# Hybrid attention trunk on one core: an attention step that takes both heads of a pair and a quarter of the tokens

## The reference, cut to what matters

```python
def nsa_mixer(...):                      # layer 0, 2 groups of 8 heads share keys
    s_c = einsum('bqghd,bngd->bghqn', qb, k_cmp); p_c = masked_softmax(s_c, cmp_end <= t)
    s_s = einsum('bqghd,bgqkd->bghqk', qb, k_s);  p_s = masked_softmax(s_s, m_s)
    s_w = einsum('bqghd,bkgd->bghqk', qb, k_w);   p_w = masked_softmax(s_w, m_w)
    o = gb[..., 0:1] * o_c + gb[..., 1:2] * o_s + gb[..., 2:3] * o_w
def dsa_mixer(...):                      # layer 1, one key and value for all 16 heads
    score = where(pos <= t, einsum('bqh,bqhs->bqs', wib, relu(qib @ ki)), NEG_INF)
    _, sel = lax.top_k(score, 256)
    s = einsum('bqhd,bqkd->bhqk', qb, k[sel]); p = masked_softmax(s, sel <= t)
    o = einsum('bhqk,bqkd->bqhd', p, v[sel])
for i in range(2):
    x = x + rms_norm(mixer(rms_norm(x, g0)), g1)
    x = x + rms_norm(conv_ffn(rms_norm(x, g2)), g3)
```

## Time and profile before

| | before |
|---|---|
| median of 3 runs | 3346.78 us (3346.12 to 3353.05) |
| the profiled execution's own time | 3344.59 us |
| its span in the profile | 3342.8 us |
| instructions in the span | 37464 |
| mean granted TensorE clock | 0.943 |

### The profile page before, as it was taken

One profiled execution on the slowest core, in us unless ns is written; L12 is line 12 of the kernel. 1 busy time (PEld: TensorE's weight loads), 2 busy tenths in 40 slices (PEclk: granted clock), 3 DMA queues, 4 the chain that ended last, 5 costly groups with the idle time before them and its releaser, 6 DMA issues.

```text
span 3342.8 us, 37464 instructions
## 1 busy us (share of the span) xinstructions
PE 2987.1 (89%) x13312; PEld 2293.7 (69%) x13312; DVE 2076.4 (62%) x3708; ACT 1512.6 (45%) x2609; POOL 278.1 (8%) x221
## 2 busy tenths in 40 slices
PE   7797999999879999999987676379997999999997
PEld 5685666666567888878865564255666788887885
DVE  6544445555166766687766699754426777667666
ACT  4342555545444444445433455444434454444443
POOL 2352000000000000000002024130000000000000
PEclk9787999999999999999998788689998999999999
DMA  5143121121332333333323012452132333333332
GB/s 167 44 105 99 43 54 41 43 49 36 101 89 76 95 99 97 95 94 96 95 70 110 7 41 87 107 140 51 33 114 69 90 96 97 96 95 95 103 103 73
DMA packets 362770, 275.17 MB, mean 82 GB/s; under 512 B 64230, under 2 KB 314152, under 8 KB 362072
## 3 DMA queue, kind: packets, MB, share of 16 engines
q1 hardware_dynamic: 361431, 270.68, 28.1%
q10 hardware_dynamic: 1152, 2.10, 0.2%
HBM read 238.18 MB, written 31.92 MB: 81 GB/s over the span
## 4 chain that ended last, share of the span: by engine, by line
PE 76%; DVE 13%; issue 4%; ACT 3%; DMA 2%; SPq 1%; POOL 0%; POOLq 0%; DVEq 0%; ACTq 0%
PE PS L490 18%; PE PS L492 18%; PE PS L491 18%; PE PS L899 10%; PE PS L822 3%; PE PS L877 3%; PE PS L875 3%; DVE m_MASK L2271 2%; PE PS L881 1%; DVE m_Z L2345 1%; DVE RT_b L595 1%; DVE m_PRED L2276 1%; PE PS L644 1%; PE PS L893 0%; DMA WR<-in_dsa_w_out 0%
## 5 line engine op out<-in xcount | busy, mean ns | idle before, releaser
L490 PE MATMUL PS<-HH,WH 128*128 128x512 f32 (+1 forms) x2160 | 857.1, 397 | 88.8 <-POOL WL L463 44.6
L491 PE MATMUL PS<-HL,WH 128*128 128x512 f32 (+1 forms) x2160 | 848.6, 393 | 0.0
L492 PE MATMUL PS<-HH,WL 128*128 128x512 f32 (+1 forms) x2160 | 847.9, 393 | 0.0
L490 PEld LDWEIGHTS PS<-HH,WH 128*128 128x128 f32 x2160 | 414.5, 192 | 183.0 <-issue 51.7
L491 PEld LDWEIGHTS PS<-HL,WH 128*128 128x128 f32 x2160 | 414.3, 192 | 86.8 <-issue 2.5
L492 PEld LDWEIGHTS PS<-HH,WL 128*128 128x128 f32 x2160 | 413.1, 191 | 86.1
L479 DVE TENSOR_TENSOR WL<-WR,WH 128x1024 fp32r<-128x1024 f32 x290 | 354.1, 1221 | 109.7 <-ACT WH L472 97.9
L472 ACT ACTIVATE WH<-WR 128x1024 fp32r<-128x1024 f32 x290 | 308.1, 1062 | 125.1 <-PE PS L492 90.0
L919 ACT ACTIVATE n_PX<-PS 128x512 f32<-128x512 f32 (+3 forms) x400 | 186.7, 468 | 257.5 <-PE PS L881 206.1
L1013 DVE CUSTOM_DVE_ANT_0 n_JUNK<-PS,n_MZ 128x512 bf16<-128x512 f32 (+2 forms) x320 | 148.7, 488 | 133.7 <-PE PS L822 131.8
L899 PE MATMUL PS<-m_PX,m_V 128*128 128x512 f32 (+3 forms) x384 | 164.4, 511 | 10.7 <-ACT m_PX L919 10.7
(11 more groups left out here) (375 smaller groups left out, 5358.2 us busy)
## 6 DMA issues: line engine op xcount, KB each, us to landing
WR<-in_ffn_w_up SPq DMA_DIRECT2D x176, 512.0 KB, 3.8
WR<-in_ffn_w_down SPq DMA_DIRECT2D x88, 512.0 KB, 3.6
WH<-qh_save SPq DMA_DIRECT2D x64, 256.0 KB
n_RB<-r_save SPq DMA_DIRECT2D x96, 128.0 KB, 3.0
WR<-in_nsa_w_out SPq DMA_DIRECT2D x16, 512.0 KB, 4.1
WL<-ql_save SPq DMA_DIRECT2D x32, 256.0 KB
WR<-in_dsa_w_in SPq DMA_DIRECT2D x16, 512.0 KB, 4.1
WR<-in_dsa_w_out SPq DMA_DIRECT2D x16, 512.0 KB, 4.1
```

The source lines that it names most:

```text
L490: nc.tensor.matmul(dst, wh, xh, start=start, stop=False)
L491: nc.tensor.matmul(dst, wh, xl, start=False, stop=False)
L492: return nc.tensor.matmul(dst, wl, xh, start=False, stop=stop)
```

## The change: what it does

A unit is now both heads of the pair, one key block, and the tokens of a quarter (256) that see it: `q` takes the place of `h`. Its scores are two runs (one per head) of `w` = 256 or 128 columns that lie side by side in one bank, so a unit has 512 or 256 columns. Queries are read as two runs 512 columns apart; a mask matmul covers the same token block of both heads (256 columns), with the identity read twice; the outputs of a quarter go to two runs of one bank. A group is a branch and a quarter. Its denominators are copied in another order, and its outputs by two copies of 64x256 in place of one of 64x512. The two DMAs of denominators go to 64 partitions each, 32 bytes to a partition, in place of 128 partitions and 16 bytes. The planner's cost goes without its floor of 0.7, and the tables of layer 1 are restated for the smaller number of steps. "cmp" units, peaks, DVE's work and the DMAs of queries, shifts and spreads are the same.

```diff
@@ -92,20 +92,21 @@
+QUARTER = HALF // 2
-def key_blocks(hf, kind):
-
-    blocks = []
-    for kb in range(4 * hf + 4):
-        low = max(kb, 4 * hf)
-        high = 4 * hf + 3 if kind == "full" else min(kb + 4, 4 * hf + 3)
-        diag = kb >= 4 * hf
-        far = kind == "near" and high == kb + 4
-        blocks.append((kb, (low - 4 * hf) * P, (high - low + 1) * P, diag, far))
-    blocks.sort(key=lambda b: b[2] < HALF)
+def key_blocks(hf, q, kind):
+
+    blocks, i0 = [], 4 * hf + 2 * q
+    for kb in range(i0 + 2):
+        low = max(kb, i0)
+        high = i0 + 1 if kind == "full" else min(kb + 4, i0 + 1)
+        if high >= low:
+            far = kind == "near" and high == kb + 4
+            blocks.append((kb, (low - i0) * P, (high - low + 1) * P, far))
+    blocks.sort(key=lambda b: b[2] < QUARTER)
...
-            cost = 3.4 if u.kind == "cmp" else max(0.7, 1.6 * u.w / HALF + dense * u.w / P)
+            cost = 3.4 if u.kind == "cmp" else 1.6 * u.w / QUARTER + dense * 2 * u.w / P
...
+        def both_heads(W, n):
+            o = n.q * QUARTER + n.c0
+            return W[:, n.r % 3, :].rearrange("p (h t) -> p h t", h=2)[:, :, o:o + n.w]
+
+        def both_parts(tile, n):
+            return tile[:, 0:2 * n.w].rearrange("p (h t) -> p h t", h=2)
...
-                nc.tensor.matmul(dst, KA[:, g, keys], query_high(n.r, n.h, n.c0, n.w),
-                                 start=True, stop=False)
-                last = nc.tensor.matmul(dst, KB[:, g, keys], query_low(n.r, n.h, n.c0, n.w),
+                nc.tensor.matmul(dst, KA[:, g, keys], both_heads(WH, n), start=True, stop=False)
+                last = nc.tensor.matmul(dst, KB[:, g, keys], both_heads(WL, n),
                                         start=False, stop=not masks)
+                ones = B["IDB"][:, :].unsqueeze(1).broadcast_to([P, 2, P])
                 for x, (ii, mask) in enumerate(masks):
                     o = ii * P - n.c0
-                    last = nc.tensor.matmul(PS[:, u % 3, o:o + P], mask, B["IDB"][:, :],
+                    last = nc.tensor.matmul(dst[:, :, o:o + P], mask, ones,
                                             start=False, stop=x == len(masks) - 1)
...
-                last = nc.tensor.matmul(PS[:, 6 + n.g % 2, n.c0:n.c0 + n.w], V[:, g, n.kb, :], probs,
+                dst = PS[:, 6 + n.g % 2, :].rearrange("p (h t) -> p h t", h=2)[:, :, n.c0:n.c0 + n.w]
+                last = nc.tensor.matmul(dst, V[:, g, n.kb, :], both_parts(B["PX"][:, u % 4, :], n),
                                         start=n.first, stop=n.last)
...
-                b, o = 6 + n.g % 2, 64 * n.h
-                nc.scalar.activation(DR[o:o + 1, slot, :], PS[64:65, b, :], ACT.Copy)
-                nc.scalar.activation(OP[o:o + 64, slot, :], PS[0:64, b, :], ACT.Copy).then_inc(a_ov, 1)
+                b, o = 6 + n.g % 2, 64 * n.q
+                nc.scalar.activation(DR[o:o + 1, slot, :].rearrange("o (p h j) -> o h p j", h=2, j=4),
+                                     PS[64:65, b, :].rearrange("o (h p j) -> o h p j", h=2, j=4), ACT.Copy)
+                for h in range(2):
+                    last = nc.scalar.activation(
+                        OP[64 * h:64 * h + 64, slot, n.q * QUARTER:(n.q + 1) * QUARTER],
+                        PS[0:64, b, h * QUARTER:(h + 1) * QUARTER], ACT.Copy)
+                last.then_inc(a_ov, 1)
...
-                    for h in range(2):
-                        sp.dma_start(a.B["R4"][:, slot, h, :],
-                                     a.B["DR"][64 * h:64 * h + 1, slot, :]).then_inc(a_chain[slot], 16)
+                    for x in range(2):
+                        row = a.B["DR"][64 * x:64 * x + 1, slot, :]
+                        if plan.units[s].kind == "cmp":
+                            sp.dma_start(a.B["R4"][:, slot, x, :], row).then_inc(a_chain[slot], 16)
+                        else:
+                            sp.dma_start(a.B["R4"][64 * x:64 * x + 64, slot, :, :],
+                                         row).then_inc(a_chain[slot], 16)
...
-        LATE_MASKS = {3: 4, 14: 5, 25: 6, 36: 7}
+        LATE_MASKS = {2: 4, 10: 5, 19: 6, 27: 7}
-        LATE_LOADS = {6 * m + 1: m for m in range(PAIRS)}
-        LATE_HIGHS = {6 * m + 9: m for m in range(PAIRS)}
-        LATE_SAVES = {6 * m + 12: m for m in range(PAIRS)}
+        LATE_LOADS = {9 * m // 2 + 1: m for m in range(PAIRS)}
+        LATE_HIGHS = {9 * m // 2 + 7: m for m in range(PAIRS)}
+        LATE_SAVES = {9 * m // 2 + 9: m for m in range(PAIRS)}
```

More of the change, by code:

```diff
@@ L94 @@
 ROUNDS = 2 * PAIRS
-Unit = namedtuple("Unit", "r kind h kb c0 w diag far first last g rb")
+QUARTER = HALF // 2
+Unit = namedtuple("Unit", "r kind q kb c0 w far first last g rb")
 Peak = namedtuple("Peak", "r kind h ii c")
-def key_blocks(hf, kind):
-    blocks = []
-    for kb in range(4 * hf + 4):
-        low = max(kb, 4 * hf)
-        high = 4 * hf + 3 if kind == "full" else min(kb + 4, 4 * hf + 3)
-        diag = kb >= 4 * hf
-        far = kind == "near" and high == kb + 4
-        blocks.append((kb, (low - 4 * hf) * P, (high - low + 1) * P, diag, far))
-    blocks.sort(key=lambda b: b[2] < HALF)
+def key_blocks(hf, q, kind):
[7 more added lines that the diff above has]
+    blocks.sort(key=lambda b: b[2] < QUARTER)
     return blocks
@@ L118, in attention_units @@
             if kind == "cmp":
-                units.append(Unit(r, kind, 0, 0, 0, HALF, False, False, True, True, groups, rb))
+                units.append(Unit(r, kind, 0, 0, 0, QUARTER, False, True, True, groups, rb))
                 groups += 2
                 continue
-            for h in range(2):
-                blocks = key_blocks(order[r][1], kind)
-                for x, (kb, c0, w, diag, far) in enumerate(blocks):
-                    units.append(Unit(r, kind, h, kb, c0, w, diag, far, x == 0, x == len(blocks) - 1,
+            for q in range(2):
+                blocks = key_blocks(order[r][1], q, kind)
+                for x, (kb, c0, w, far) in enumerate(blocks):
+                    units.append(Unit(r, kind, q, kb, c0, w, far, x == 0, x == len(blocks) - 1,
                                       groups, rb))
@@ L850, in scores_pe @@
                 pe.wait_ge(a_ex, a.qk0 + u - 2)
-            dst = PS[:, u % 3, 0:n.w]
             if n.kind == "cmp":
+                dst = bank(u % 3)
                 for h in range(2):
@@ L863, in scores_pe @@
             else:
+                dst = both_parts(PS[:, u % 3, :], n)
                 KA, KB = (B[x] for x in a.keys[n.kind][0:2])
@@ L867, in scores_pe @@
                 for ii in range(n.c0 // P, (n.c0 + n.w) // P):
-                    i = 4 * hf + ii
+                    i = 4 * hf + 2 * n.q + ii
                     if "MASK" in B and i >= 2:
@@ L888, in values_pe @@
             pe.wait_ge(a_ex, a.qk0 + u + 1)
-            probs = B["PX"][:, u % 4, 0:n.w]
             if n.kind == "cmp":
+                probs = B["PX"][:, u % 4, :]
                 if n.g:
@@ L918, in exp_act @@
                 act.wait_ge(a_pv, a.qk0 + u - 3)
-            nc.scalar.activation(a.B["PX"][:, u % 4, 0:n.w], PS[:, u % 3, 0:n.w],
+            nc.scalar.activation(a.B["PX"][:, u % 4, 0:2 * n.w], PS[:, u % 3, 0:2 * n.w],
                                  ACT.Exp).then_inc(a_ex, 1)
@@ L933, in evict_act @@
             act.wait_ge(a_pv, a.qk0 + u + 1)
-            if n.h == 0 and n.rb >= a.ns:
+            if n.q == 0 and n.rb >= a.ns:
                 act.wait_ge(a_tm, a.rb0 + n.rb - a.ns + 1)
```

## The result

The changed kernel takes **3311.4 us** (median of four runs, 3309.4 to 3314.2) against 3346.7 for the kernel before beside it: ratio 0.9891, 95% interval 0.9874 to 0.9908. In a later series of runs the same kernel gave 3315.3 against 3346.4, ratio 0.9905 (0.9891 to 0.9918). So it is 31 to 36 us faster, where 20 were forecast. The median lies at the low end of the forecast's range (3311), and by the first ratio the kernel stands at 3310.3, just under it.

A forecast was written before the change was run, and what follows sets the result against it. PE was taken to bound most of attention, with ACT and DVE in its shadow. Terms -18 + 2.7 - 4.3 + 0 = -20 us against the profiled 3344.6 gave 3324.6, median 3327 us; range 3311 to 3343.

The forecast's parts named there:

- seam: Matmuls that read or write two runs: taken as free; rival that it costs 19 ns each gives 3357 us, chance 0.10.
- -18 for steps: Layer 0: fewer steps and mask turns save 2.3 us per pair, 18 us for eight, ends 15 and 23.
- +2.7 for evictions: Layer 0: each group's eviction grows by 170 ns, bare only at 16 places before "cmp"; low end 0.
- I take 0.02 off each: Layer 0: 20 masked steps per pair that stay have shorter turns to f32 weights, 0.4 us a pair.
- a step costs 0.05 us beyond its columns: PE in attention: a step without a mask takes 1.33 us, of which columns make 1.28.
- PE's waits: Layer 0: a pair goes from 70.7 to about 68.7 us, by -2.3 for steps and +0.34 for evictions.
- -4.3 forecast: Layer 1, second half: two steps less and 14 shorter turns, 0.54 us per round, eight rounds; ends 2 and 8.
- Nothing else in it waits: Layer 1, second half: no waits beside the steps that are priced, so only 0.54 us per round falls.
- the ring: Layer 1, first half: it holds three peaks; bunching turns a burst of 8 into 12, up to 2.2 us more.
- over 118 us: Sign to check: if layer 1's first half takes longer than this, the ring is the cause.
- I take 0: Layer 1, first half: 2 us saved by sixteen fewer steps set against the ring; net nothing, between -5 and +6.
- as many issues ... nothing: SP and DMAs: the number of issues stays and no wait in the steady pairs hangs on them, so no time.

The follow-up runs named there:

- inter: The changed kernel with the two heads interleaved column by column in a unit: 3307.2 us, ratio 0.9880.
- m128: The changed kernel with each 256-column mask matmul issued as two of 128 columns, one per head: 3330.8 us, ratio 0.9949.
- s128: The changed kernel with the score matmuls of the 256-column units only issued per head, 128 columns each: 3338.3 us, ratio 0.9971.
- evict4: The changed kernel with the two output copies of a group's eviction issued as four of 64x128: ratio 0.9912.
- ring35: The changed kernel with layer 1's peaks allowed 3.5 us (planner's time) after the round that frees their slot, in place of 5.0: 3315.6 us, ratio 0.9903.
- bbunch: The kernel before with layer 1's peaks allowed 7.0 us (planner's time) after the round that frees their slot, in place of 5.0: 3348.3 us, ratio 1.0006.

## Why the prediction was right or wrong

- **Direction, records, seam.** Right: 888 records less, plain step 1.33. (The near branch of a second half has 2560 score columns of each head, which "1280 or 3328" leaves out; the forecast's totals hold them.) The sentence of the Trainium skill that the forecast weighed ("PSUM — Partial Sum Buffer", Specifications: any access pattern that is not contiguous slows matmuls significantly) is not borne out here: not by masks written to PSUM in two runs (the masked step takes 1.33 us, its columns alone 1.28), nor by values written as single elements 1 KB apart (inter, 1.29).
- **Layer 0: -18 for steps and +2.7 for evictions forecast, -31 measured.** Three steps of the forecast failed. First, "I take 0.02 off each" for the mask turns that stay: m128 gives 0.048, 0.96 a pair where 0.4 stood, 4.5 us in all. Second, "a step costs 0.05 us beyond its columns" was taken from full steps; the high scores of a 128-column unit cost 0.05 more, ten a pair, 4 us in all by s128's price. The earlier trace rows had the hint: the masked step's 0.06 came from a 53-ns stream in front of a 193-ns load, and score streams of 128 columns stand there too. Together PE's busy time fell by 3.35 us a pair where 2.3 were forecast. Third, PE's waits: forecast 0.34 longer a pair, measured 0.58 shorter, 7 us in all. The three add up to the missing 16 us.
- **Layer 1, second half: -4.3 forecast, -17.5 measured.** "Nothing else in it waits" was false: the earlier trace rows has 25.90 - 24.82 = 1.08 us a round without PE. It was the wait at the transpose, and it went, for 7.6 us. PE's busy time fell by 1.26 us a round where 0.54 was forecast; m128 gives 0.78 of it, and the high scores of two narrow units 0.1.
- **Eviction: +2.7 forecast, +1.4** by evict4: L955 took 376 ns and L952 590, as forecast, but it is bare once a pair. The wait behind L943 at a pair's first "cmp" was 1.30 us before and 1.27 after.
- **Layer 1, first half: 0 forecast, between -5 and +6; +10.5 measured.** The forecast's own sign for the ring, over 118 us, came up at 124.9, and ring35 gives back 6.6 of the 7.4 us between rounds 0 and 7; bbunch says that bunches do so only in the shorter rounds, if they do. So "I take 0" for the ring may be the step that failed, or "as many issues ... nothing" for SP, whose count stayed and whose order changed: the cause stays open. What failed for certain is leaving the clock out: of the 7.4 us waits gave +5.5, the clock +5, work -3. The other 3 us stand about round 0 and were not traced.
- **The search: nothing forecast, +5.4**, by another phase between VectorE and GpSimd.
- **Luck.** The measured time came out within a microsecond of the range's end although most of the terms were off, because the losses (+10.5 and +5.4) hid half of what attention gained beyond the forecast.

## What to carry to other kernels

Price a stream by what stands behind it, not by its columns alone: here 128 columns in front of an f32 weight load cost 0.05 us more than their columns, 256 columns under 5 ns more, and a 128-column mask with another bf16 mask behind it next to nothing. Subtract busy time from length before you write that nothing waits: the row that was to be shortened held 1.08 us of wait. When steps become fewer, print for each engine and queue what now falls on the same step; a count that stays says nothing of the order. Where PE waits much, give the clock a term of its own, from rows at both levels, and do not take it as a share of the waits.

## What was not expected of the hardware

- A step whose scores read f32 elements 2 KB apart and whose values were written 1 KB apart took 1.29 us, against 1.33 with contiguous ones.
- A 107-ns stream hid an f32 weight load whose record is 193 ns long, and a 53-ns stream fell short by 0.05 us.
- By windows of one us, PE's clock fell to 0.5 after a gap four times in the stretch before, for 3 to 7 us each, and five times in the changed kernel, for 3 to 10 us; with the masks short the waits fell by 10 us in one kernel and by 6 in the other, and the loss to the clock by about 1 in both.
- A 6-element VectorE operation of 0.17 us took 1.15 to 1.8 us beside GpSimd's 512-column ones, tensor_scalar with a column as scalar too, and a search of the same code took 63.5, 68.9 or 75 us by its phase to them.
